# Six of the 96 loads of expert weights issued as 112, 8 and 8 partitions instead of 128

## The reference, cut to what matters

```python
D_MODEL, N_EXPERTS, D_EXPERT, CAP_FACTOR = 1024, 16, 1024, 2

def expert_choice_ffn(h, w_router, w_gate_up, w_down):
    B, N, D = h.shape
    cap = CAP_FACTOR * N // N_EXPERTS
    aff = jax.nn.softmax((h @ w_router).astype(jnp.float32), axis=-1)
    g, idx = lax.top_k(jnp.swapaxes(aff, 1, 2), cap)
    xs = jax.vmap(lambda hb, ib: hb[ib])(h, idx)
    gu = jnp.einsum('becd,edf->becf', xs, w_gate_up)
    gate, up = jnp.split(gu, 2, axis=-1)
    y = jnp.einsum('becf,efd->becd', jax.nn.silu(gate) * up, w_down) * g[..., None].astype(h.dtype)
    return jax.vmap(lambda ib, yb: jnp.zeros((N, D), yb.dtype).at[ib.reshape(-1)].add(yb.reshape(-1, D)))(idx, y)
```

## Time and profile before

| | us |
|---|---|
| median of 3 runs | 893.77 |
| lowest and highest | 891.56, 894.37 |
| the profiled execution | 892.39 |
| its span, first to last instruction | 890.6 |

### The profile page before, as it was taken

The page is one execution under the profiler, slowest core; times in us unless marked ns, Lnnn a source line. Parts: engine busy times, 40 slices in busy tenths (PEclk is TensorE's granted clock), DMA queues, the critical chain, the costliest instruction groups (busy, mean ns, idle before and its releaser), DMA issues.

```text
span 890.6 us, 16597 instructions
## 1 busy us (share of the span) xinstructions
PE 833.6 (94%) x7235; PEld 434.1 (49%) x7235; DVE 606.0 (68%) x1028; ACT 218.8 (25%) x397; POOL 77.9 (9%) x111
## 2 busy tenths in 40 slices
PE   6889999799899988999999999999999899999994
PEld 5779978466678877333333333322222222222232
DVE  4669656789879886486855865685584575585286
ACT  2374456856741330000110010010010010010023
POOL 0010310001011011201101100110110110100001
PEclk9999999899999999999999999999999999999998
DMA  9941550441048379999999999999999999999975
GB/s 331 387 160 45 218 192 1 190 149 44 2 177 312 150 302 359 371 414 393 417 396 390 407 409 387 387 423 392 391 417 398 389 427 385 386 419 419 414 314 118
DMA packets 37588, 273.37 MB, mean 307 GB/s; under 512 B 5208, under 2 KB 5516, under 8 KB 25228
## 3 DMA queue, kind: packets, MB, share of 16 engines
q1 hardware_dynamic: 29168, 245.97, 68.4%
q0 software_dynamic: 7440, 23.67, 9.5%
q10 hardware_dynamic: 908, 2.68, 0.8%
HBM read 259.68 MB, written 14.19 MB: 308 GB/s over the span
## 4 chain that ended last, share of the span: by engine, by line
PE 61%; DMA 23%; DVE 8%; ACT 5%; issue 2%; SPq 1%; DVEq 0%; ACTq 0%
PE PS L1399 17%; DMA wr<-in_w_gate_up 11%; PE PS L1402 9%; PE PS L1416 9%; DMA wr<-in_w_down 8%; PE PS L1425 4%; PE PS L989 4%; PE PS L991 4%; PE PS L990 4%; PE PS L1204 2%; PE PS L1188 2%; DMA ring<-in_w_mod 2%; DMA w_qkv<-in_w_in 2%; PE PS L1227 1%; PE PS L1158 1%
## 5 line engine op out<-in xcount | busy, mean ns | idle before, releaser
L1399 PE MATMUL PS<-wr,XT 128*32 128x512 f32 x2048 | 246.5, 595 | 5.7 <-DMA wr<-in_w_gate_up 5.5
L1399 PEld LDWEIGHTS PS<-wr,XT 128*32 128x32 f32 x2048 | 72.8, 110 | 154.5 <-issue 139.3
L1402 PE MATMUL PS<-wr,XT 128*32 128x512 f32 x1024 | 135.4, 594 | 0.0
L1416 PE MATMUL PS<-wr,HT 128*32 128x512 f32 x1024 | 122.2, 593 | 7.0 <-DMA wr<-in_w_down 7.0
L1946 DVE TENSOR_TENSOR h_s<-gate_s,PS 128x512 f32<-128x512 f32 x16 | 11.0, 687 | 160.7 <-ACT gate_s L920 160.7
L1937 DVE STREAM_TRANSPOSE XT<-Xg 32x256 f32<-32x256 f32 x180 | 115.1, 639 | 2.6
L920 ACT ACTIVATE gate_s<-PS 128x512 f32<-128x512 f32 x16 | 9.6, 598 | 318.3 <-PE PS L1402 318.3
L1962 DVE STREAM_TRANSPOSE HT<-h_s 32x256 f32<-32x256 f32 x128 | 82.0, 640 | 1.5
L1416 PEld LDWEIGHTS PS<-wr,HT 128*32 128x32 f32 x1024 | 35.2, 110 | 82.4 <-issue 64.1
L1402 PEld LDWEIGHTS PS<-wr,XT 128*32 128x32 f32 x1024 | 37.0, 111 | 73.7 <-issue 73.7
L989 PE MATMUL PS<-WAh,Hh 128*128 128x512 f32 (+1 forms) x168 | 61.5, 366 | 4.9 <-DVE Hl L1547 3.2
(11 more groups left out here) (322 smaller groups left out, 1109.7 us busy)
## 6 DMA issues: line engine op xcount, KB each, us to landing
wr<-in_w_gate_up SPq DMA_DIRECT2D x64, 2048.0 KB, 30.0
wr<-in_w_down SPq DMA_DIRECT2D x32, 2048.0 KB, 31.4
ring<-in_w_mod SPq DMA_DIRECT2D x24, 1024.0 KB, 10.2
ring<-in_w_in SPq DMA_DIRECT2D x4, 1024.0 KB, 11.5
ring<-in_w_out SPq DMA_DIRECT2D x4, 1024.0 KB, 6.5
w_qkv<-in_w_in SPq DMA_DIRECT2D x4, 768.0 KB, 14.4
h_scratch<-h POOLq DMA_DIRECT2D x5, 512.0 KB, 5.3
acc_scratch<-xt POOLq DMA_DIRECT2D x5, 512.0 KB, 5.9
```

Source lines behind the costliest of these rows:

```text
L1399: pe.matmul(PS[32 * j:32 * j + 32, 512 * b:512 * b + 512], x[:, 32 * (j % 2):32 * (j % 2) + 32], w[:, lo + 512 * (j // 2):lo + 512 * (j // ...
L1402: last = pe.matmul(PS[32 * j:32 * j + 32, 512 * bp:512 * bp + 512], x[:, CAP_S:SLQ], w[:, 512 * j:512 * j + 512], start=(k == 0), stop=(k ...
L1416: last = pe.matmul(PS[32 * j:32 * j + 32, 512 * bs:512 * bs + 512], HT[e % 2][:, f, 32 * (j % 2):32 * (j % 2) + 32], w[:, lo + 512 * (j // ...
```

## The change

Pairs 24, 36, 48, 60, 72 and 84 are loaded by three DMAs: partitions 0 to 111, then 112 to 119, then 120 to 127. Each adds 16 to the buffer's semaphore, so such a load adds 48, and PE's wait takes its value from `pair_in`, which adds up 16 or 48 per load of this buffer.

```diff
+PARTS = {n: 3 for n in range(24, 96, 12)}
+
+def pair_in(n):
+    return 16 * sum(PARTS.get(m, 1) for m in range(n % NSLOT, n + 1, NSLOT))
@@
-            sp.dma_start(wr[s][:], (w_gu_v if kind == "gu" else w_dn_v)[e][:, k // 2, :]).then_inc(w_in_slot[s], 16)
+            w_in = (w_gu_v if kind == "gu" else w_dn_v)[e][:, k // 2, :]
+            if n in PARTS:
+                for lo, hi in ((0, 112), (112, 120), (120, 128)):
+                    sp.dma_start(wr[s][lo:hi, :], w_in[lo:hi, :]).then_inc(w_in_slot[s], 16)
+            else:
+                sp.dma_start(wr[s][:], w_in).then_inc(w_in_slot[s], 16)
@@
             if n % 2 == 0:
-                pe.wait_ge(w_in_slot[s], 16 * (n // 2 // NSLOT + 1))
+                pe.wait_ge(w_in_slot[s], pair_in(n // 2))
```

## The result

| | us |
|---|---|
| before, median of 4 runs | 892.83 |
| changed, median of 4 runs | 967.01 |
| lowest and highest | 961.6, 970.83 |
| ratio, with its 95% interval | 1.0818 [1.0785, 1.0851] |
| the profiled execution | 965.21 |

The change makes the kernel 74 us slower, 12.4 us for each of the six split loads. 897.4 was forecast, and 898.9 was the top of the range.

What follows compares the result with a forecast made beforehand. From 581 to 839 us the landing of weights, set by the slowest DMA engine, was taken to bound the kernel. Six extra packets of 0.612 us, 3.67 us, on the median 893.77 gave 897.4 us, range 892.8 to 898.9.

Steps and rivals of the forecast that it cites:

- the price of a packet: 16 KB packets in the weight stream: 161.4 us of engine time for 263 large packets, so 0.61 us each.
- +0.61 us for F, six times: +3.7: Each split pair: eight favoured DMA engines carry 9 packets, the other eight 7; over six pairs +3.7 us.
- F: The eight DMA engines assumed to take both 8-partition pieces of each split pair: 9 packets against 7.
- The bounds: Extra time on the favoured engines: 0 if pieces take turns, 3.9 us with completions, +7.3 us if 14 engines carry 112.
- The counts of packets: Split pair on SP's queue: 112 partitions as 7 packets on each of 16 engines, each 8 as one on eight engines.
- a delay anywhere after pair 24: DMA engines never run dry: a packet added there delays all that follows on its engine, even before PE waits.
- The slowest engine in F: Likeliest case, at the weights' end: the latest engine is among the favoured eight, +3.7 us, 897.4 us, chance 0.45.
- slowest engine in G: Rival: latest engine among the other eight, so the slowest late favoured one decides; -0.5 to +2.5 us, 895.0, chance 0.33.
- The 15.4 us: PE's stall between pairs 44 and 91: 47 pairs took 257.5 us instead of 242.0, 0.33 us per pair.
- It costs nothing as long as the weights are late anyway: PE's clock lowered by longer stalls: free where PE catches up in the next stall, up to 1.4 us at pair 91.
- The rival that came out faster: Ninth engine late only at the tail, other late ones not favoured: landings 3.7 us earlier, 890.1 us, chance 0.09.
- the one without a shift: Rival: second piece of 8 goes to the other eight engines, each again 8 packets: 893.8 us, chance 0.09.

Runs made afterwards that it cites:

- spare_own: Kernel before plus, behind each of six pairs, two unread loads of 8 partitions by 12 KB, to each fourth of partitions 0 to 31: 898.55 us.
- columns: Changed kernel with the six pairs halved by columns instead, all 128 partitions in each of two loads: 893.66 us, ratio 1.0009.
- half_own: Changed kernel, six pairs load only partitions 0 to 63, as eight loads of each fourth partition of 0 to 31 or 32 to 63: 895.12 us.
- one_split: Changed kernel with only pair 24 split into 112, 8 and 8 partitions: 901.52 us, ratio 1.0086.
- spare_other: Kernel before plus, behind each of six pairs, two unread loads of 8 partitions by 12 KB, to each fourth of partitions 64 to 95: 910.34 us.

## Why the prediction was wrong

**The step that failed** is the price of a packet. "A packet of 16 KB takes 0.61 us" was read from loads of 128 partitions and put on all packets of the new loads. In the dips it is 1.2 us, and up to 1.7 us. The term "+0.61 us for F, six times: +3.7" was right for more packets on F in own places, as spare_own shows (4.4 us measured where this working gives 5.5). The change moves the place too, and that is worth 20 times as much.

**The bounds were too narrow for the same reason.** They spanned the ways to deal packets (0 to +7.3 us), but none the duration of a packet in a shape that the trace didn't hold. The nearest row was the load of 8 partitions, of which I used the count alone. A count of packets says nothing of how long one takes. Shapes other than 128 partitions had no price, and the range should have said so.

**Splitting a load** was priced by its packets and issues alone, as if it did not matter how the load is cut. It does: 64 + 64 costs 48 us over six loads. Where the parts keep all 128 partitions, as in `columns`, a split costs at most 2 us over six loads.

**Point by point.** The counts of packets: right as far as the trace goes. The whole kernel's SP queue, before:

```profile
q1 hardware_dynamic: 29168, 245.97, 68.4%
```

It has 29264 after, 96 more, which is 6 x (16 + 8 + 8 - 16) completions: 16 engines for the 112 partitions and 8 for each piece of 8. Were 112 dealt to 14 engines, it would be 84. The issues on SP, 0.33 us each, cost nothing: right, as `columns` shows for one issue more per pair and `half_own` for seven more. That a delay anywhere after pair 24 counts in full, also where PE had not yet waited: right (one_split). The slowest engine in F: F's packets count nearly in full, if F takes all small pieces (half_own, spare_own), but the 4.4 us of spare_own, 2.9 to 5.9 by its interval, would also fit a slowest engine in G with one of F up to 2.6 us behind.

The 15.4 us for which PE "stands still" from 581.23 to 838.70 us were misread. The profile's waits for weights in that stretch are 10.9 us (12.5 less the first, 1.6), and the slow matmuls at 708.97 are 1.4 more (3.30 us in place of 1.90, at a granted clock of 0.56). "It costs nothing as long as the weights are late anyway", of PE's clock, holds for the slow matmuls that another stall follows. Behind the last stall of a slow stretch it is wrong, as the prediction itself said of the last wait of all, and that came five times, 7.6 us. The rival that came out faster and the one without a shift stand against +8.2%.

## What to carry to other kernels

Load 128 partitions at once where the DMA engines are the bound; if a load must be split, split it by columns (893.7 us) and not by partitions (941.9 us for halves). Pieces of 8 partitions did no harm of their own when they took each fourth of partitions 0 to 31 or 32 to 63 (895.1 us with eight such pieces for half a pair, 938.3 us with blocks); each fourth of 64 to 95 did (910.3 us, spare_other). A slice with full DMA engines but fewer GB/s (256 in place of some 400) had slow packets here (1.2 to 1.7 us in place of 0.61): look at the shapes of the transfers that it carries, and those of the neighbours in the queue.

## What the runs showed of the hardware that I had not expected

- The partitions that a load writes decide its speed, and not those that it reads: 893.0 us for own places from blocks, 935.3 us for blocks from own places.
- The damage isn't confined to the odd load. 2 x 96 KB of extra loads outside own places take the rate of all loads from 430 to 352 GB/s over 15 us, and in the changed kernel 720 or more packets of whole loads took 1 us or more, beside the 768 of the split ones.
- Stalls of 3 to 5 us each halved PE's clock (0.50 from 541 to 544 us) for all or part of the 16 matmuls behind them, which took 2.5 to 3.6 us in place of 1.9. PE was busy 22.8 us longer by it, but only the 7.6 us behind the last stall of each slow stretch are on the chain of work; the rest took the place of waiting.
